# One stage of two-job rounds for the first mixer's projections: a prediction from the profile

## The reference

```python
u = rms_norm(h, g_mix[i]) @ w_in[i]
q_lat, kv_lat, k_rope, qd, kd, vd = jnp.split(u, IN_OFFSETS, axis=-1)   # 256, 128, 32, 512, 512, 512
# mla_mixer
q = (rms_norm(q_lat, g_q_lat) @ w_q_up).reshape(B, S, 8, 64 + 32)
kv = (rms_norm(kv_lat, g_kv_lat) @ w_kv_up).reshape(B, S, 8, 64 + 64)
k_nope, v = kv[..., :64], kv[..., 64:]
q_nope = rms_norm(q[..., :64], g_q[:64])
q_rot = apply_rope(rms_norm(q[..., 64:], g_q[64:]), cos, sin)
k_nope = rms_norm(k_nope, g_k[:64])
k_rot = apply_rope(rms_norm(k_rope, g_k[64:]), cos, sin)
# diff_mixer: 4 heads, two halves of 64 each
q = rms_norm(qd.reshape(B, S, 4, 2, 64), g_q)
k = rms_norm(kd.reshape(B, S, 4, 2, 64), g_k)
lam = exp(sum(lq1 * lk1)) - exp(sum(lq2 * lk2)) + lambda_init
```

## Time and profile before

| what | value |
|---|---|
| median of 3 runs | 2925.09 us (2917.99 to 2927.91) |
| the profiled execution | 2925.36 us |
| its span, from the first to the last instruction | 2923.5 us |
| mean granted clock of TensorE | 0.916 |
| first latent product | 503.7 us |
| first job from the latents | 554.4 us |
| first differential job | 634.2 us |
| end of the second stage | 746.9 us |

### The profile page before, as it was taken

How to read it: one execution, slowest core, us unless ns; L and a number is a source line. 1 busy time by engine, 2 the same in 40 slices (tenths; PEclk the granted TensorE clock), 3 DMA queues, 4 the chain that set the end, 5 groups by cost and what they waited for, 6 DMA issues and landing times. The chain is left out here.

```text
span 2923.5 us, 22452 instructions
## 1 busy us (share of the span) xinstructions
PE 2516.5 (86%) x8621; PEld 1326.1 (45%) x8621; DVE 547.8 (19%) x1083; ACT 439.7 (15%) x741; POOL 49.1 (2%) x76
## 2 busy tenths in 40 slices
PE   7999999668978999999988998779999758887783
PEld 3444444224744444444436785446886433332231
DVE  1000001220552100000121114874000130010012
ACT  1000001344342100000021003432000100000003
POOL 0000000000000000000000000000000000000001
PEclk9999999879989999999999996778999769899997
DMA  3232322012001522232113210000233229999995
GB/s 99 72 83 74 88 70 66 18 29 57 15 1 30 186 77 80 72 88 79 48 44 89 67 51 22 1 1 1 65 120 126 88 96 426 431 430 430 431 430 234
DMA packets 248407, 359.25 MB, mean 123 GB/s; under 512 B 15985, under 2 KB 224497, under 8 KB 236066
## 3 DMA queue, kind: packets, MB, share of 16 engines
q1 hardware_dynamic: 239840, 326.90, 31.7%
q0 software_dynamic: 5600, 21.10, 1.8%
q10 hardware_dynamic: 2914, 10.56, 0.9%
HBM read 337.49 MB, written 21.04 MB: 123 GB/s over the span
## 5 line engine op out<-in xcount | busy, mean ns | idle before, releaser
L397 PE MATMUL PS<-M 128*128 128x512 f32 x1408 | 608.0, 595 | 7.4 <-DVE M L325 7.4
L2264 PE MATMUL PS<-M 128*64 128x512 f32 x1536 | 373.2, 642 | 98.5 <-DMA M<-w 76.4
L350 PE MATMUL PS<-M 128*128 128x512 f32 x960 | 415.6, 595 | 12.8 <-POOLq L259 6.6
L397 PEld LDWEIGHTS PS<-M 128*128 128x128 f32 x1408 | 268.6, 191 | 346.9 <-issue 344.0
L70 PE MATMUL PS<-M 128*128 128x264 f32 (+1 forms) x1544 | 371.9, 404 | 33.6 <-ACT M L314 19.1
L70 PEld LDWEIGHTS PS<-M 128*128 128x128 f32 x1544 | 295.9, 193 | 109.4 <-issue 27.2
L350 PEld LDWEIGHTS PS<-M 128*128 128x128 f32 x960 | 183.0, 191 | 245.4 <-issue 244.4
L2264 PEld LDWEIGHTS PS<-M 128*64 128x64 f32 x1536 | 127.2, 147 | 333.0 <-issue 307.7
L424 DVE TENSOR_TENSOR M<-M,PS 128x512 f32 x44 | 30.2, 688 | 570.6 <-PE PS L397 570.6
L412 ACT ACTIVATE M<-PS 128x512 f32<-128x512 f32 x44 | 26.3, 597 | 568.7 <-PE PS L397 568.7
L2330 DVE TENSOR_TENSOR M<-M,PS 128x512 f32<-128x512 f32 x16 | 11.0, 689 | 444.0 <-PE PS L2264 444.0
(11 more groups left out here) (323 smaller groups left out, 1894.4 us busy)
## 6 DMA issues: line engine op xcount, KB each, us to landing
M<-w SPq DMA_DIRECT2D x96, 2048.0 KB, 18.7
M<-w_ffn_gate SPq DMA_DIRECT2D x44, 512.0 KB, 4.0
M<-w_ffn_up SPq DMA_DIRECT2D x44, 512.0 KB, 5.2
M<-w_ffn_down SPq DMA_DIRECT2D x16, 1408.0 KB, 6.9
M<-w_in SPq DMA_DIRECT2D x41, 512.0 KB, 3.9
expert_rows<-M POOLq DMA_DIRECT2D x2, 4096.0 KB, 18.2
expert_rows<-M ACTq DMA_DIRECT2D x16, 512.0 KB, 10.3
M<-w_in SPq DMA_DIRECT2D x5, 1024.0 KB, 5.5
```

The lines of the kernel that those rows point to most:

```text
L350: last = nc.tensor.matmul(PS[:, 4 + k, :], slot(s, 0, tiles, P)[:, a, :], rhs(a), start=a == 0, stop=a == tiles - 1)
L397: last = nc.tensor.matmul(PS[:, 2 * k + half, :], slot(s, half * KD * P, KD, P)[:, a, :], xnT[:, a, 0:S1], start=a == 0, stop=a == KD - 1)
L2264: last = nc.tensor.matmul(PS[ROWS * k:ROWS * k + ROWS, bank, :], wide[:, a * P + ROWS * k:a * P + ROWS * k + ROWS], weights(k), start=star ...
```

## The change

The two stages become one, `proj1_pe`, `proj1_act`, `proj1_dve`, without the barrier between them. All 18 jobs stand in nine rounds of two, written out, heavy ones (differential, 8 products a job) among light ones (q and rope 2 products, k 1 product). Three pairs of banks, 6/7, 0/1 and 2/3, take turns for the projections. TensorE projects round r + 1 before it sums round r. The first differential job is projected between the latents and their sums. ScalarE squares round r + 1 before it takes the roots of round r, and takes both Ln of a round and then both Exp. `SQ` and `RS` have two sets of two. `w_q_up` and `w_kv_up` have places of their own outside the ring, `WQ` and `WKV`, and their loads, with that of `dist` and the two latent chunks, are sent before SP waits for the end of the feed-forward stage. Both differential chunks of a head share one slot. The value projection fills a whole bank of 512 columns for each tile of tokens, from both slots, and so ScalarE copies it in four instructions rather than eight. POOL, and the stage numbers that SP waits for later, count one barrier less.

The diff, cut to its core (the removed functions are those printed above):

```diff
@@ sizes and rounds
-PLE_STAGE = 9
-PROJ2_STAGE = 13
+PLE_STAGE = 8
+PROJ2_STAGE = 12
+        WQ, WKV = at(WORK0 + 27648, 2, 768), at(WORK0 + 29184, D)
+        T3 = at(WORK0 + 30208, 2, S1)
+        ROUNDS = [diff_pair(0), diff_pair(1), query_jobs((0, 1)), query_jobs((2, 3)), diff_pair(2), rope_jobs(),
+                  key_jobs((0, 1)), diff_pair(3), key_jobs((2, 3))]
+        ROPE_ROUND = 5
+
+        def round_bank(r):
+
+            return (6, 0, 2)[r % 3]
@@ TensorE
+            def project(r, k):
+                job = ROUNDS[r][k]
+                bank = round_bank(r) + k
+                if r >= 3:
+                    pe.wait_ge(j_out, 2 * (r - 3) + k + 1)
+                elif r > 0:
+                    pe.wait_ge(lat_x, 1)
...
+            def sums(r):
+                if r > 0:
+                    pe.wait_ge(j_rs, 2 * r)
+                if r == ROPE_ROUND + 1:
+                    pe.wait_ge(j_out, 2 * r)
+                for k, job in enumerate(ROUNDS[r]):
+                    pe.wait_ge(j_sq, 2 * r + k + 1)
+                    last = nc.tensor.matmul(PS[:, 4 + k, :], C[job["groups"]], SQ[:, 2 * (r % 2) + k, :], start=True,
+                                            stop=True)
+                    if k == 0 and r in chunk_of:
+                        last.then_inc(w_used[chunk_of[r][0]], 1)
+                last.then_inc(j_ss, 1)
+
+            project(0, 0)
             pe.wait_ge(lat_sq, 4)
...
+            project(0, 1)
             pe.wait_ge(lat_x, 1)
...
+            for r in range(len(ROUNDS)):
+                if r + 1 < len(ROUNDS):
+                    if r + 1 == 2:
+                        pe.wait_ge(lat_done, 1)
+                    for k in range(2):
+                        project(r + 1, k)
+                sums(r)
+                if r == ROPE_ROUND:
+                    for k in range(2):
+                        pe.wait_ge(j_x, k + 1)
+                        nc.tensor.matmul(PS[:, 4 + k, :], C["rot32"], T1[:, k, :], start=True,
+                                         stop=True).then_inc(j_rot, 1)
+            for t in range(4):
+                bank = round_bank(9 + t // 2) + t % 2
+                pe.wait_ge(j_out, 2 * (6 + t // 2) + t % 2 + 1)
...
+            chunks = [ring.chunk() for c in range(2)]
+            for t in range(4):
+                bank = round_bank(11 + t // 2) + t % 2
+                if t < 2:
+                    pe.wait_ge(j_out, 16 + t + 1)
+                else:
+                    pe.wait_ge(v_free, t - 1)
@@ ScalarE
+            def squares(r):
+                for k in range(2):
+                    act.wait_ge(j_proj, 2 * r + k + 1)
+                    if k == 0 and r >= 2:
+                        act.wait_ge(j_ss, r - 1)
+                    nc.scalar.activation(SQ[:, 2 * (r % 2) + k, :], PS[:, round_bank(r) + k, :],
+                                         ACT.Square).then_inc(j_sq, 1)
+
+            def roots(r):
+                nc.scalar.preload_act_table_set(LN)
+                act.wait_ge(j_ss, r + 1)
+                if r < 2:
+                    act.wait_ge(lat_x, 1)
+                else:
+                    act.wait_ge(j_out, 2 * r - 2)
+                for k, job in enumerate(ROUNDS[r]):
+                    nc.scalar.activation(RS[:, 2 * (r % 2) + k, :], PS[:, 4 + k, :], ACT.Ln, bias=eps_col,
+                                         scale=1.0 / job["width"])
+                act.drain()
+                for k in range(2):
+                    rs = RS[:, 2 * (r % 2) + k, :]
+                    nc.scalar.activation(rs, rs, ACT.Exp, scale=-0.5).then_inc(j_rs, 1)
+
+            squares(0)
+            for r in range(len(ROUNDS)):
+                if r + 1 < len(ROUNDS):
+                    squares(r + 1)
+                roots(r)
@@ VectorE
+            for r, jobs in enumerate(ROUNDS):
+                rope = r == ROPE_ROUND
                 for k, job in enumerate(jobs):
+                    dve.wait_ge(j_rs, 2 * r + k + 1)
+                    for lo, hi, dest in ([(0, P, T1[:, k, :])] if rope else job["dests"]):
+                        last = nc.vector.scalar_tensor_tensor(dest, PS[lo:hi, round_bank(r) + k, :], job["gain"][lo:hi],
+                                                              RS[lo:hi, 2 * (r % 2) + k, :], ALU.mult, ALU.mult)
+                    last.then_inc(j_x if rope else j_out, 1)
@@ SyncE
-            sp.wait_ge(stage_done, WORKERS * 2)
-            sp.dma_start(cos1, I["c_cos1"]).then_inc(tables_in, 16)
-            sp.dma_start(sin1, I["c_sin1"]).then_inc(tables_in, 16)
+            sp.dma_start(WQ, I["w_q_up"].rearrange("(a p) n -> p a n", p=P)).then_inc(wqkv_in, 16)
+            sp.dma_start(WKV, I["w_kv_up"]).then_inc(wqkv_in, 16)
             sp.dma_start(dist, I["c_dist"]).then_inc(tables_in, 16)
...
+            sp.wait_ge(stage_done, WORKERS * 2)
+            sp.dma_start(cos1, I["c_cos1"]).then_inc(tables_in, 16)
+            sp.dma_start(sin1, I["c_sin1"]).then_inc(tables_in, 16)
+            for h in range(4):
+                s, ready, use = ring.chunk(2)
+                sp.wait_ge(w_used[s], use)
+                for k in range(2):
+                    lo = 416 + 512 * k + h * P
+                    sp.dma_start(slot(s, k * KD * P, KD, P), w_in[:, :, lo:lo + P]).then_inc(w_ready[s], 16)
@@ GpSimd
-            stage(pool, "pool"); stage(pool, "pool")
+            stage(pool, "pool")
             diff_bias_pool(pool); stage(pool, "pool")
```

More of the change, by code:

```diff
@@ L493, in lat_pe @@
             nc.tensor.matmul(PS[:, 5, :], ones, SQ[:, 2, :], start=True, stop=True)
[L494 removed]
+            nc.tensor.matmul(PS[32:64, 3, :], ones[0:32, 0:32], SQ[0:32, 3, :], start=True, stop=True).then_inc(lat_ss, 1)
+            project(0, 1)
             pe.wait_ge(lat_x, 1)
[L496 removed]
+            nc.tensor.matmul(PS[64:96, 3, :], C["rot32"][0:32, 0:32], krope[0:32, :],
@@ new lines, in proj1_pe @@
+            for t in range(4):
+                bank = round_bank(9 + t // 2) + t % 2
+                pe.wait_ge(j_out, 2 * (6 + t // 2) + t % 2 + 1)
+                nc.tensor.matmul(PS[:, bank, :], kvlat[:, t * P:(t + 1) * P], WKV[:, 512:1024], start=True,
+                                 stop=True).then_inc(v_ready, 1)
+            chunks = [ring.chunk() for c in range(2)]
[3 more added lines that the diff above has]
+                    pe.wait_ge(j_out, 16 + t + 1)
+                else:
+                    pe.wait_ge(v_free, t - 1)
+                for c, (s, ready, _) in enumerate(chunks):
+                    pe.wait_ge(w_ready[s], ready)
+                    for a in range(KD):
+                        last = nc.tensor.matmul(PS[:, bank, 256 * c:256 * c + 256], xnT[:, a, t * P:(t + 1) * P],
+                                                slot(s, 0, KD, 256)[:, a, :], start=a == 0, stop=a == KD - 1)
+                last.then_inc(v_ready, 1)
@@ L500, in lat_act, with proj1_act @@
+            for s, _, _ in chunks:
+                pe.drain().then_inc(w_used[s], 1)
+        def proj1_act(act):
             ring = rings["act"]
@@ L507, in lat_act @@
             act.wait_ge(lat_ss, 1)
-            for n, (buf, bank, m, width) in enumerate(LAT):
-                nc.scalar.activation(RS[0:m, buf, :], PS[0:m, 4 + n, :], ACT.Ln, bias=eps_col[0:m], scale=1.0 / width)
+            for buf, bank, (lo, hi), width in LAT:
+                nc.scalar.activation(RS[0:hi - lo, buf, :], PS[lo:hi, bank, :], ACT.Ln, bias=eps_col[lo:hi],
+                                     scale=1.0 / width)
             act.drain()
-            for buf, bank, m, width in LAT:
-                last = nc.scalar.activation(RS[0:m, buf, :], RS[0:m, buf, :], ACT.Exp, scale=-0.5)
+            for buf, bank, (lo, hi), width in LAT:
+                last = nc.scalar.activation(RS[0:hi - lo, buf, :], RS[0:hi - lo, buf, :], ACT.Exp, scale=-0.5)
@@ L516, in lat_dve, with proj1_dve @@
+            for dmas in (2, 2, 2, 2, 1, 1):
+                ring.chunk(dmas)
+        def proj1_dve(dve):
             ring = rings["dve"]
-            ring.chunk(), ring.chunk()
+            for dmas in (1, 1, 2, 2, 2, 2, 1, 1):
+                ring.chunk(dmas)
             for n in range(2):
@@ L524, in lat_dve @@
             dve.drain().then_inc(lam_dot, 1)
+            for gain in (g["mla_q_nope"], g["mla_q_rope"]):
+                nc.vector.tensor_scalar(gain, gain, MLA_SCALE, None, ALU.mult)
+            dve.drain()
             dve.wait_ge(lat_rs, 1)
@@ L565, in job_act @@
[L565 to L575, removed]
@@ L596, in mla_jobs @@
[L596 to L617, removed]
@@ L619, in program @@
[L619 to L634, removed]
-                pe.wait_ge(v_free, k)
-                last = nc.tensor.matmul(PS[:, 2 + (k - 1) % 2, :], kvlat[:, t * P:(t + 1) * P], values,
-                                        start=True, stop=True)
-                last.then_inc(v_ready, 1)
-            pe.drain().then_inc(w_used[sq_], 1)
```

(16 more changed lines are left out.)

179 lines of the change are left out of this document (50 added, 129 removed).

## The result

| what | before | after |
|---|---|---|
| median | 2924.69 us (2917.99 to 2927.91, 4 runs) | 2851.82 us (2846.18 to 2862.58, 4 runs) |
| ratio | 1 | 0.9758, 95% interval 0.9725 to 0.9792 |
| span of the profiled execution | 2923.5 us | 2849.5 us |
| first latent product | 503.7 us | 499.5 us |
| end of the stage | 746.9 us | 675.6 us |

The ratio is the changed kernel's time over that of the kernel before. The kernel is 72.9 us faster. The profiled spans differ by 74.0 us: 67.1 of them lie in the stretch that was rewritten, 4.2 ahead of it and 2.7 behind. The 4.2 us are no effect of the change.

A forecast was written before the change was run, and what follows sets the result against it. TensorE's waits and lower clock, 94.4 of the stage's 243.2 us, were all the change could touch. The ledger moved stage end from 746.9 to 679.6, so 2925.4 - 67.3 = 2858 us; small errors 2848 to 2868, high end 2880.

The forecast's parts named there:

- the ledger: Running account of TensorE's time through the new stage: 676.6 us at full clock, 679.6 with 3 us for the clock.
- The latents: Latent products at the stage's start: 29.4 us, to 533.2, as before; earlier loading of the first weights costed at nothing.
- ScalarE's pace: In the nine rounds, squares, two loads, Ln, Exp and hand-overs take 6.4 us a round, setting the light rounds' pace.
- The clock: TensorE's low clock after two longer waits, before the rotations and the sums of round 8: 3 us.
- The head: First differential jobs and sums cover the latents' 7.6 us chain, leaving 0.8 us waited; round 1's products cover the additions.
- Transfers at nothing: Weight loads for the stage all hidden, with 3 us at the least; w_q_up, w_kv_up and dist hidden by 3.5 us.
- The rope wait: TensorE stands some 5 us before the two rotations, with round 7 issued only behind them.
- Table loads: Loads fall from 36 to 18, priced at 1.28 us each; by the page's 2.66 us, some 18 us more in all.
- A: Rival: light rounds run at 1.2 GHz, 27 us more, time 2882; chance 0.12 wholly or half.
- B: Rival: ScalarE's share is bigger, loads stay at four a round, 18 us more, time 2876; chance 0.04.
- C: Rival: new waits (rope wait, late weight chunks) replace the barrier's, 35 us, 2893 at worst; chance 0.03 with something unseen.
- D: Rival: slower, TensorE's low clock in the whole stage, ending near 811, time 2989; chance 0.02.

The follow-up runs named there:

- the bare head: Changed kernel with both jobs of round 0 projected only after the latents' chain and its eight additions: 2873.22 us, ratio 0.9833.
- the run with late loads: Changed kernel with w_q_up, w_kv_up, dist and both latent chunks sent only after the feed-forward stage's end: 2855.02 us, ratio 0.977.
- the kernel with rotations between: Changed kernel with the rope round's two rotations placed between the two jobs of round 7: 2848.37 us, ratio 0.9746.
- four loads: Changed kernel with ScalarE taking Ln and Exp of each job separately, four table loads a round rather than two: 2878.97 us, ratio 0.9855.
- the lookahead: Undone in the changed kernel by projecting round r + 1 only after VectorE has written round r: 2906.86 us, ratio 0.9944.
- the tail's order: Kernel with rotations between, plus V1 tiles 0 and 1 before the last sums and differential values reordered: 2845.30 us, again 2841.60 us.
- the kernel with heavy rounds last: Changed kernel with one heavy round first, then the five light ones, then the other three heavy ones: 2863.85 us, ratio 0.9805.

## Why the prediction was right, point by point

Forecast 2858, measured 2851.8 (and 2855.4 the second time). The forecast for the stage was 175.9 us from the first product (503.7 to 679.6), the two traces have 176.1 and 177.5. The 6 us by which 2851.8 lies under the forecast are outside the stage, 4.2 ahead of it and 2.7 behind. Set on the trace's own start (everything moved by 4.2 us), the ledger compares so:

| point of the ledger | forecast | after + 4.2 |
|---|---|---|
| round 0 summed | 567.5 | 566.7 |
| roots 0 | 571.8 | 570.7 |
| roots 2 | 584.6 | 582.8 |
| sums of round 3 | 595.6 | 594.2 |
| rotations done | 614.5 | 615.9 |
| round 6 summed | 629.9 | 632.5 |
| value projection begins | 647.8 | 651.2 |
| stage end, with 3 us for the clock | 679.6 | 679.8 |

- *The latents.* 29.4 us forecast from the row of before, 27.8 measured: the first products met the full clock this time. In the second profile of the same kernel they ran at a mean of 0.95, and the stage took 177.5.
- *ScalarE's pace.* 6.4 us forecast, 6.05 measured; the two squares and the two Exp overlap more than I had from rows of single ones. Some 2 us over seven rounds.
- *The clock.* Mis-sized: 3 us forecast. Against the same groups at full clock, the sums of round 5 cost 1.7 us more (3.68 against 1.98), the rotations 1.9, the start of round 7 1.2 (15.10 against 13.90), and the sums of round 8 1.8 (3.78 against 1.98), 6.6 in all. I had not counted on the low clock after the 2.35 us wait before the sums of round 5. (V1's four products were slow too, 4.92 in place of 3.60, but the value projection waited for VectorE behind them.) Pace and latents offset it, and that the end fits to 0.2 us is luck.
- *The head.* The wait for the scaled latents was 0.8 us forecast and 0.75 measured; that cover of 20.2 us is what the bare head shows.
- *Transfers at nothing.* Held; the run with late loads shows no gain from the early ones either. No load ended a wait of TensorE in this stage. The row of the last w_ffn_down weights did not start late either: TensorE works from 439.63 to 487.00 without a wait. The forecast put that load and the three sent behind it at 15.4 us by the rate of one alone; they took 11.4 (449.41 to 460.8).
- *The rope wait.* Forecast as the one new wait of note, some 5 us; 4.1 measured, and removable as the kernel with rotations between shows.
- *Table loads.* The Trainium skill ("ScalarE: Activation LUTs", section What ACT_TABLE_LOAD costs) has 2.66 us with the drain. Here a load of 1.28 us was followed at once by its Ln (567.46 to 568.75), so the row and not the page's sum was the price.
- *Rivals.* A in two places only, 6.6 us of its 27. B fell, two loads a round; its price of 18 us was too low, since four loads cost 25.0 with TensorE's slow sums. C and D fell here; C's late weight chunk did come, with 4.95 us, where the heavy rounds stand together. The rule of "TensorE: Matmul & The Clock Gate", section HAM oscillation, in the Trainium skill agrees with the waits of 4.12 and 4.06 us, each followed by 3.78 us for four instructions, and with four loads a round, where a wait of 3.50 us was followed by slow sums. It doesn't tell apart the waits of 2.35 and 2.33 us (last section).

What the prediction did not say is how the gain divides. Undone one by one, the loads cost 25.0 us, the lookahead 52.3, the head 20.2 and the order 5.4 (through other waits than the one it was meant to show): 102.9 us for a gain of 67.1. The parts are no sum. Most waits that come back also bring the low clock, and the loads alone, put into the old order, were worth 3.9.

## What to carry to other kernels

A shorter chain helps only where something overlaps with it: fewer table loads gave 3.9 us while the next pair hung on the last one's result, and their loss cost 25 once the next round was in flight. So first take the wait away (other banks, the next projection ahead of this one's sums), then shorten the engine that sets the pace. In a hand-written order look for the instruction that waits with heavy independent work queued behind it, and put it between two pieces of that work; here this and the tail's order gave 13.8 us. Before heavy jobs are moved together, count the weight slots: with two slots the third heavy round in a row waited 4.95 us for its load.

## What the runs showed of the hardware that I had not expected

Price a pause twice: the same four sums took 1.98 us after waits of about 0.6 us and 3.58 to 3.68 us in two places after waits of 3.50 and 2.35 us. Where they lie in another engine's chain, its period grows by this too (6.05 to 10.3 us a round, with 2.6 us of loads). But the length of the pause does not settle it. In the changed kernel the sums of round 7 waited 2.33 us, as long as those of round 5, and ran at the full clock; in the kernel with heavy rounds last they did so after 4.00 us (585.02, above):

```profile
632.32 1.98 PE L555 MATMUL PS<-M 128*128 128x512 f32 x4 [2.33 <-ACT M L644]
```

It was the same in the second profile of the changed kernel (3.66 us after 2.34, 1.98 after 2.33). TensorE had worked without a wait from 611.46 to 630.0 before the pause that cost nothing; before the other, from 574.39 to 593.4, then had a wait of 0.61 and 3.7 us of work. What decides between them is not shown.

Transfers were faster together than alone. 1408 KB alone landed in 6.9 us, 209 GB/s. By the same measure, from the first issue to the last landing, the 3904 KB of the kernel with late loads took 12.8 us (491.4 to 504.1), 313 GB/s. At its best its queue ran at 417 GB/s, as this view of its DMA between 480 and 510 us shows in 40 slices; in the view of the load alone no slice is above 350:

```profile
GB/s 0 0 0 0 0 0 0 0 0 0 0 0 0 0 0 0 78 147 389 406 411 417 416 367 389 356 345 348 363 383 385 131 22 0 0 0 0 0 0 11
```
